# Two output projections of a fused eight-block transformer stack: five outputs over seven feature blocks beside the last mixer, their eighth block inside the sixth output

## The chip, the cores and the metric
The kernel runs on one core of a Trainium2 chip. The core has a matrix engine (TensorE, PE in the profile; its weight loads are PEld), a vector engine (VectorE, DVE), a scalar engine (ScalarE, ACT) and GpSimd (POOL); SyncE (SP) issues the DMAs. Engines run their own instruction streams in order and wait for one another by semaphores. The metric is the device time of one execution in microseconds; lower is better.

## What is computed
Two models of two layers follow one another on 512 latent tokens of width 1024. All data are kept with features on the 128 partitions, in KC = 8 feature blocks of 128, and tokens along the free axis. The part around the change is the first model:

```
layer 0:  x_lat += g1 * (attention(h_lat, h_ctx) @ na_w_o)      # 512 latent and 256 context tokens
          x_ctx += cg1 * (attention_ctx(h_ctx) @ na_w_o)
          x_lat += g2 * swiglu(norm(x_lat)), x_ctx likewise
layer 1:  x_lat += g1 * (readout(gated scans of h) @ hg_w_o)    # latent only from here
          x_lat += g2 * swiglu(norm(x_lat))
```

The attention has 16 heads, taken in eight pairs; a pair yields one feature block of 128 of the attention's output (o_lat, o_ctx). The second mixer has 8 heads of 128, and each yields one feature block of y_lat. So the input blocks of each output projection become ready one after the other, and the last one only when the last mixer is done.

## The kernel before
A weight matrix is taken in pieces. A piece is one block of 128 output features over kn feature blocks of the input (kn = 8 in most); its weights are one DMA of 512 KB into a ring of three w_raw buffers. Each product is computed with a high and a low part of both operands: ACT casts w_raw to w_high (event `w`, L1185), DVE subtracts to get w_low (L1514), and per feature block PE makes three products with 512 latent columns (L914 to L916) and, where there is context, three with 256 (L919 to L921). w_high and w_low are rings of two, by the piece's number: ACT's cast for piece n waits until piece n-2 and all before are done (`s_mm`).

The order of the work is written out by a planner, the class `Schedule`, as one list of events; every engine walks the same list and does its share of each event. `piece` first lays down the preload of its own weights, then the products of the piece before it (which were staged), and stages its own. The epilogue of a piece (event `epi`) comes behind the second block of the next piece's products, followed by an adaptive-modulation row (`ada`, two DVE products of 128x1024 with the weights of another DMA, L1526), one per piece in layer 0. `preload(2)` converts the first two pieces of the next stage in advance. `flush` lays down what is staged, with its epilogue.

Mixers are generators. `start_background(mixer, slots)` lets a mixer with a given number of steps be spread evenly over so many slots; each feature block but the first of a piece is a slot (`tick`), and a step is put behind its products. `end_background` lays down all steps that are left, one after the other. The attention mixer of a pair has 32 steps (transposes of v, the norms of q and k, nine empty ones, then five rounds of scores, transposes of the probabilities and value products), the second mixer 34 (gates, logarithms, scans, then seven levels of a decomposition of the scores: differences on POOL, exponentials on ACT, products on DVE, score products on PE three levels later; then the output and its norm).

In both mixer stages the mixer of head i lies beside the pieces of head i+1: 21 slots for the 32 attention steps, 35 for the 34 of the second. The last attention mixer starts when nothing is left beside it, so that all its steps are laid down by `end_background`. The last one of the second stage starts behind its second forget-gate piece with a rate of 34 steps in 28 slots; 14 slots are there (pieces v and g), the other half of the steps comes behind.

Then come `preload(2)`, eight events `to_h` (ACT casts block k of o_lat and o_ctx, or of y_lat, into h_high, L1224, L1225, L1228; DVE subtracts to h_low, L1573, L1575, L1578) and the eight output pieces. Their epilogue adds gate times product to x_lat and x_ctx on DVE (L1588, L1590), and `feed` adds ACT's squares (`sq`) and POOL's running sum of them (L1951) for the next norm. `flush`, `preload(2)` and `norm` follow: `ssum` (PE, L944 for the running sum and L947 for the last square), `rstd` (ACT), and per block the modulation and the split into h_high and h_low (L1560, L1166, L1566), which the first FFN products wait for.

Of the kernel before, what the change touches and what calls it, by code (L numbers as in the profile page):

```python
# [59 lines left out]

TABLES = {ACT.Exp: "natural_log_exp_and_others", ACT.Ln: "natural_log_exp_and_others", ACT.Silu: "silu_and_others",
# [3 lines left out]
class Piece:  # L65


    def __init__(self, src, kn, rhs, epi, gate):
        self.src, self.kn, self.rhs, self.epi, self.gate = src, kn, rhs, epi, gate
        self.ctx = rhs in ("hc", "uc")  # L70


class Schedule:
# [81 lines left out]
    def piece(self, src, kn, rhs, epi, gate=None, first=False, then=None):  # L155
        n = len(self.pieces)
        self.pieces.append(Piece(src, kn, rhs, epi, gate))
        if n >= self.loaded:
            self.preload()

        def products():
            if first:
                self.run_epilogues()
            for k in range(kn):
                self.ev("mm", n, k)
                if k == 1:
                    self.run_epilogues()
                    self.flush_late()
                    self.fill_ada(self.ada_rate)
                if k >= 1:  # L170
                    self.tick()
            self.pending.append(finish)
# [213 lines left out]
    def main(self):  # L386
# [8 lines left out]
        self.interleave([self.na_pieces(i) for i in range(KC)], [(self.na_mixer(i), 32) for i in range(KC)], 3 * (KC - 1))  # L395
        self.preload(2)
        for k in range(KC):
            self.ev("to_h", 0, k)
        for m in range(KC):
            self.piece(io["na_o"][m], KC, "hc", ("res", m, 0, 2, 1), gate=("to_h", 0) if m == 0 else None)  # L400
        self.flush()
        self.preload(2)
# [7 lines left out]
                        tail_chunks=4 * (KC - 1), after=2)  # L410
        self.preload(2)
        for k in range(KC):
            self.ev("to_h", 1, k)
        for m in range(KC):
            self.piece(io["hg_o"][m], KC, "h", ("res", m, 1, 2, 3), gate=("to_h", 1) if m == 0 else None)
        self.flush()
        self.preload(2)
# [37 lines left out]
def build(nc, io):  # L455
    ctx = ExitStack()
    with ctx:
# [128 lines left out]
        s_th, s_tl = sem("s_o_high"), sem("s_o_low")  # L586
        s_uh, s_ul = sem("s_u_high"), sem("s_u_low")
# [29 lines left out]
        by_epi = {p.epi: n for n, p in enumerate(pieces)}  # L617

# [41 lines left out]


# [32 lines left out]
        def mix_uses(ev):  # L694
            kind = ev[0]
            v = nth[ev]
            if kind == "shm":
                return []
            if kind == "shift":
# [100 lines left out]
        def _(e):  # L800
# [19 lines left out]
            for ev in plan:  # L820
                kind = ev[0]
                if kind == "w":
# [3 lines left out]
                    e.dma_start(raw[slot][:, 0:p.kn * P], p.src).then_inc(s_raw[slot], 16)  # L826
# [48 lines left out]
        def _(e):  # L875
# [6 lines left out]
            for ev in plan:  # L882
# [41 lines left out]

                elif kind == "shift":
# [231 lines left out]
        def _(e):  # L1157
# [10 lines left out]
            for ev in plan:  # L1168
# [17 lines left out]
                elif kind == "sq":  # L1186
# [4 lines left out]
                    else:  # L1191
                        n = by_epi[("res", k, *RES_OF[s], s)]
                        e.wait_ge(*(ctx_free if HAS_CTX[s] else lat_free)[n])
# [26 lines left out]
                elif kind == "to_h":  # L1220
                    _, which, k = ev
                    if which == 0:
# [278 lines left out]
        def _(e):  # L1501
# [5 lines left out]
            for ev in plan:  # L1507
# [71 lines left out]

                elif kind == "epi":  # L1580
# [541 lines left out]
```

## Time and profile before

| | us |
|---|---|
| median of 3 runs | 3602.36 (3601.1 to 3602.77) |
| the profiled execution | 3599.17 |
| its span | 3597.4 |
| PE busy in it | 3328.5 |
| DVE busy | 1747.3 |
| ACT busy | 1273.6 |
| POOL busy | 399.4 |
| weight products over h (L914 alone, 2752 of them) | 1136.0 |

The chain that ended last is PE for 80% of the span, DVE for 7%, ACT for 5%, POOL for 4%. The mean granted clock of PE is 0.974 of full speed. A matmul's duration in the rows contains its latency; back to back, its successor starts earlier than it ends. A row of the timeline gives the start, the duration, the engine, the line, output and inputs, and in brackets how long the engine was idle before it and what ended that.

### The profile page before, as it was taken

The page shows a single profiled execution, that of the slowest core. Times are in us where ns is not written, and L with a number is a line of the kernel's source. Part 1 is how long each engine was busy: PE and PEld are TensorE (multiplying, and loading weights), DVE is VectorE, ACT ScalarE, POOL GpSimd, SP SyncE. Part 2 cuts the span into 40 slices and gives each one's busy share as a digit, 9 for nine tenths or more (in the row PEclk, how much of TensorE's full clock was granted, in tenths as well). Part 3 has the DMA queues.
Part 4 walks back from the last instruction along what each step waited for, and adds up shares of the span by engine and source line. Part 5 has one row for each costly group of instructions (what it writes and reads, how often), then busy time and mean ns, then how long its engine had stood idle before and what let it go on. Part 6 is the DMA issues. An engine that isn't in the chain of part 4 may idle for free.

```text
span 3597.4 us, 42857 instructions
## 1 busy us (share of the span) xinstructions
PE 3328.5 (93%) x17064; PEld 2756.1 (77%) x17064; DVE 1747.3 (49%) x2602; ACT 1273.6 (35%) x1965; POOL 399.4 (11%) x400
## 2 busy tenths in 40 slices
PE   3888878999999999997999999999989999999898
PEld 3777757888887778776788878887768788877686
DVE  3666667755533676765533334343333333433333
ACT  2444443212123465554322233333332333333322
POOL 1011001000001253533000000001100000011000
PEclk7999999999999999998999999999999999999999
DMA  5322213665621211111333322222223222222132
GB/s 175 86 68 64 68 47 112 193 195 191 194 91 47 64 48 48 48 42 43 101 94 95 93 96 70 76 74 79 69 67 100 91 81 72 69 83 76 53 97 85
DMA packets 107974, 318.75 MB, mean 89 GB/s; under 512 B 28160, under 2 KB 29568, under 8 KB 107264
## 3 DMA queue, kind: packets, MB, share of 16 engines
q1 hardware_dynamic: 107776, 316.00, 28.3%
q8 instruction: 137, 2.24, 0.3%
q14 instruction: 61, 0.50, 0.0%
HBM read 313.86 MB, written 2.10 MB: 88 GB/s over the span
## 4 chain that ended last, share of the span: by engine, by line
PE 80%; DVE 7%; ACT 5%; POOL 4%; issue 3%; DMA 1%; SPq 0%; DVEq 0%; ACTq 0%
PE bank L914 20%; PE bank L916 20%; PE bank L915 20%; PE bank L919 3%; PE bank L921 3%; PE bank L920 3%; PE bank L1108 1%; DVE tmp L1560 1%; PE bank L1127 1%; PE bank L1137 1%; POOL hg_d L1994 1%; ACT L1165 1%; PE bank L1009 1%; POOL hg_d L1995 1%; PE bank L982 1%
## 5 line engine op out<-in xcount | busy, mean ns | idle before, releaser
L914 PE MATMUL bank<-h_high_lat,w_high 128*128 128x512 f32 x2752 | 1136.0, 413 | 84.5 <-DVE h_low_ctx L1566 34.6
L1514 DVE TENSOR_TENSOR w_low<-w_raw,w_high 128x1024 fp32r<-128x1024 f32 (+2 forms) x440 | 537.3, 1222 | 1125.2 <-ACT w_high L1185 1123.8
L916 PE MATMUL bank<-h_high_lat,w_low 128*128 128x512 f32 x2752 | 1082.6, 393 | 0.0
L915 PE MATMUL bank<-h_low_lat,w_high 128*128 128x512 f32 x2752 | 1082.5, 393 | 0.0
L1185 ACT CAST w_high<-w_raw 128x1024 fp32r<-128x1024 f32 (+2 forms) x440 | 451.1, 1027 | 1335.0 <-PE bank L916 858.8
L914 PEld LDWEIGHTS bank<-h_high_lat,w_high 128*128 128x128 f32 x2752 | 523.0, 190 | 195.7 <-issue 63.6
L916 PEld LDWEIGHTS bank<-h_high_lat,w_low 128*128 128x128 f32 x2752 | 522.4, 190 | 113.1
L915 PEld LDWEIGHTS bank<-h_low_lat,w_high 128*128 128x128 f32 x2752 | 524.6, 191 | 79.3 <-issue 8.2
L1526 DVE SCALAR_TENSOR_TENSOR ada_product<-w_raw,c_rows 128x1024 f32<-128x1024 f32 x192 | 246.0, 1281 | 65.5 <-DMA w_raw<-in_ada_w_dram 53.8
L1951 POOL TENSOR_TENSOR rstd<-rstd,square 128x512 f32<-128x512 f32 (+1 forms) x42 | 64.8, 1544 | 1496.9 <-ACT square L1166 1496.6
L919 PE MATMUL bank<-h_high_ctx,w_high 128*128 128x256 f32 x800 | 225.6, 282 | 0.0
L920 PE MATMUL bank<-h_low_ctx,w_high 128*128 128x256 f32 x800 | 225.5, 282 | 0.0
L921 PE MATMUL bank<-h_high_ctx,w_low 128*128 128x256 f32 x800 | 225.3, 282 | 0.0
L919 PEld LDWEIGHTS bank<-h_high_ctx,w_high 128*128 128x128 f32 x800 | 151.2, 189 | 33.1
L920 PEld LDWEIGHTS bank<-h_low_ctx,w_high 128*128 128x128 f32 x800 | 151.2, 189 | 32.9
L921 PEld LDWEIGHTS bank<-h_high_ctx,w_low 128*128 128x128 f32 x800 | 153.8, 192 | 0.0
L916 PE MATMUL bank<-u_high_lat,w_low 128*128 128x512 f32 x352 | 139.0, 395 | 0.0
L915 PE MATMUL bank<-u_low_lat,w_high 128*128 128x512 f32 x352 | 138.9, 395 | 0.0
L914 PE MATMUL bank<-u_high_lat,w_high 128*128 128x512 f32 x352 | 138.3, 393 | 0.4 <-DVE u_low_lat L1610 0.4
L2006 POOL TENSOR_TENSOR ret_rot<-head_in,cos 128x512 f32<-128x512 f32 x16 | 23.4, 1461 | 974.7 <-DVE ya_low L1886 689.1
L1166 ACT ACTIVATE na_p<-bank,na_stat 128x512 f32<-128x512 f32 (+1 forms) x96 | 58.9, 616 | 150.0 <-DVE na_stat L1678 131.1
L1165 ACT ACT_TABLE_LOAD x64 | 82.1, 1283 | 71.1 <-DVE att_stat L1864 48.8
(244 smaller groups left out, 4285.4 us busy)
## 6 DMA issues: line engine op xcount, KB each, us to landing
w_raw<-in_w_in_dram SPq DMA_DIRECT2D x176, 512.0 KB, 3.5
w_raw<-in_ada_w_dram SPq DMA_DIRECT2D x88, 512.0 KB, 3.9
w_raw<-in_ffn_in_dram SPq DMA_DIRECT2D x88, 512.0 KB, 3.6
w_raw<-in_w_ada_dram SPq DMA_DIRECT2D x48, 512.0 KB, 4.5
w_raw<-in_hg_in_dram SPq DMA_DIRECT2D x40, 512.0 KB, 3.5
w_raw<-in_ffn_out_dram SPq DMA_DIRECT2D x32, 512.0 KB, 3.6
w_raw<-in_qkv_dram SPq DMA_DIRECT2D x24, 512.0 KB, 3.6
w_raw<-in_proj_ret_dram SPq DMA_DIRECT2D x16, 512.0 KB, 3.5
```

The source lines that it names most:

```text
L914: e.matmul(lat_b, a, h[:, k, :], start=start, stop=False)
L915: e.matmul(lat_b, a, l[:, k, :], start=False, stop=False)
L916: done = e.matmul(lat_b, b, h[:, k, :], start=False, stop=stop)
L919: e.matmul(ctx_b, a, h[:, k, :], start=start, stop=False)
L920: e.matmul(ctx_b, a, l[:, k, :], start=False, stop=False)
L921: done = e.matmul(ctx_b, b, h[:, k, :], start=False, stop=stop)
L1165: e.preload_act_table_set(name)
L1166: return e.activation(out, in_, func, **kw)
L1185: e.copy(w_hi[n % 2][:, 0:p.kn * P], raw[slot][:, 0:p.kn * P]).then_inc(s_hi, 1)
L1514: e.tensor_tensor(w_lo[n % 2][:, 0:w], raw[slot][:, 0:w], w_hi[n % 2][:, 0:w].bitcast(F32), ALU.subtract).then_inc(s_lo, 1)
L1526: e.scalar_tensor_tensor(ada_x[:, :], raw[slot][:, :], 1.0, cb[:, c, :], ALU.mult, ALU.mult, accum_out=mod[layer][:, idx, k, c:c + 1]).the ...
L1951: e.tensor_tensor(RS[:, 0:w], RS[:, 0:w], sqr[(k - 1) % 2][:, 0:w], ALU.add).then_inc(s_gadd, 1)
```

## The change
Both projections now have three parts. `project` lays down the first five outputs (EARLY = 5) as pieces over the first seven feature blocks; they are the tail of the mixer stage, and the last mixer is spread over their slots (30 in the first projection; 44 in the second, which are the 14 of before and 30). Their `to_h` events for blocks 0 to 6 stand ahead of them, behind the last piece of the mixer stage, and ACT waits before the first until that piece is done, since h_high is its input. The epilogues add the seven-block sums to x as usual, but feed no squares.

`project_last` then ends the mixer, lays down `to_h` for block 7 and computes the sixth output over all eight blocks. The eighth weight blocks of outputs 0 to 4 are one piece of their own, loaded by one DMA of runs of 128 numbers. Behind blocks 2 to 6 of the sixth output stands one event `last` each: the three (in the first projection six) products of block 7 for one of the five outputs, into a mixer bank, and DVE's add of the result to x_lat (and x_ctx), followed by the squares of that output. Behind the fifth, the weights of the seventh output are preloaded. Outputs 7 and 8 follow, with `preload(2)` ahead of the last output's products instead of behind them.

```diff
+EARLY = 5
@@ interleave
-    def interleave(self, producers, mixers, chunks, tail=(), tail_chunks=0, after=-1):
+    def interleave(self, producers, mixers, chunks, tail=(), tail_chunks=0, after=-1, keep=False):
...
             for p in tail:
                 p()
-            self.end_background()
+            if not keep:
+                self.end_background()
             return
...
+    def project(self, which):
+        W, layer = (self.io["na_o"], 0) if which == 0 else (self.io["hg_o"], 1)
+
+        def early(m):
+            if m == 0:
+                self.preload()
+                self.flush()
+                for k in range(KC - 1):
+                    self.ev("to_h", which, k)
+            self.piece(W[m, :, 0:(KC - 1) * P], KC - 1, "hc" if which == 0 else "h", ("res", m, layer, 2, None),
+                       gate=("to_h", which) if m == 0 else None)
+
+        return [lambda m=m: early(m) for m in range(EARLY)]
+
+    def project_last(self, which, s):
+        W, layer = (self.io["na_o"], 0) if which == 0 else (self.io["hg_o"], 1)
+        rhs = "hc" if which == 0 else "h"
+        n = len(self.pieces)
+        self.pieces.append(Piece(W[0:EARLY, :, (KC - 1) * P:KC * P].rearrange("m p c -> p m c"), EARLY, rhs, ("last", which), None))
+        self.preload()
+        self.flush()
+        self.preload()
+        self.end_background()
+        self.ev("to_h", which, KC - 1)
+
+        def between(k):
+            m = k - 2
+            if 0 <= m < EARLY:
+                self.ev("last", which, m, n)
+                self.feed(s, m)
+            if m == EARLY - 1:
+                self.preload()
+
+        self.piece(W[EARLY], KC, rhs, ("res", EARLY, layer, 2, s), between=between)
+        self.staged.pop(0)()
+        for m in range(EARLY + 1, KC):
+            self.piece(W[m], KC, rhs, ("res", m, layer, 2, s))
+        self.preload(2)
+        self.flush()
@@ main, first projection
-        self.interleave([self.na_pieces(i) for i in range(KC)], [(self.na_mixer(i), 32) for i in range(KC)], 3 * (KC - 1))
-        self.preload(2)
-        for k in range(KC):
-            self.ev("to_h", 0, k)
-        for m in range(KC):
-            self.piece(io["na_o"][m], KC, "hc", ("res", m, 0, 2, 1), gate=("to_h", 0) if m == 0 else None)
-        self.flush()
-        self.preload(2)
+        self.interleave([self.na_pieces(i) for i in range(KC)], [(self.na_mixer(i), 32) for i in range(KC)], 3 * (KC - 1),
+                        tail=self.project(0), tail_chunks=5 * (KC - 2), keep=True)
+        self.project_last(0, 1)
@@ main, second projection
-                        tail_chunks=4 * (KC - 1), after=2)
...
+                        tail=self.project(1), tail_chunks=2 * (KC - 1) + 5 * (KC - 2), after=2, keep=True)
+        self.project_last(1, 3)
@@ PE
+                elif kind == "last":
+                    _, which, m, n = ev
+                    a, b = w_hi[n % 2][:, m * P:(m + 1) * P], w_lo[n % 2][:, m * P:(m + 1) * P]
+                    if m == 0:
+                        e.wait_ge(s_lo, n + 1)
+                        e.wait_ge(s_tl, 2 * KC if which == 0 else 3 * KC)
...
+                    done.then_inc(s_last if m < EARLY - 1 else s_mm, 1)
@@ ACT, to_h
+                    if k == 0:
+                        e.wait_ge(s_mm, to_h_from[which])
@@ DVE
+                elif kind == "last":
+                    _, which, m, n = ev
+                    layer = which
+                    e.wait_ge(s_mod, mod_nth[(layer, 2)])
+                    e.wait_ge(*((s_last, (EARLY - 1) * which + m + 1) if m < EARLY - 1 else (s_mm, n + 1)))
+                    e.wait_ge(*lat_free[by_epi[("res", m, layer, 2, None)]])
+                    e.scalar_tensor_tensor(XL[:, m, :], mix_bank[(ev, 0)][:, :], mod[layer][:, 2, m, 0:1], XL[:, m, :],
+                                           ALU.mult, ALU.add).then_inc(s_ll, 1)
...
```

## Rows read from the trace of the kernel before

**Rows 1.** The page: busy time, share of the span, instructions.
```profile
PE 3328.5 (93%) x17064; PEld 2756.1 (77%) x17064; DVE 1747.3 (49%) x2602; ACT 1273.6 (35%) x1965; POOL 399.4 (11%) x400
```

**Rows 2.** Copies that close a head: all by line, and one in the timeline.
```profile
L1697 DVE COPY o_ctx<-bank x8: 424/425/425, 169.2 to 518.6; 128x256 f32<-128x256 f32 x8
...
477.85 0.42 DVE L1697 COPY o_ctx<-bank 128x256 f32<-128x256 f32 x1 [2.73 <-PE bank L1009]
...
L1809 DVE SCALAR_TENSOR_TENSOR y_lat<-tmp,vectors,rstd x8: 751/752/754, 1254.8 to 1653.6; 128x512 f32<-128x512 f32 x8
```

**Rows 3.** Windows: length, busy PE, PEld, DVE, ACT, POOL, PE's clock, DMA.
```profile
428.70:469.90 41.20, 36.55 (x250) 29.76 (x249) 28.24 (x59) 17.31 (x37) 5.14 (x7) 1.00 0.16 38
477.70:522.40 44.70, 25.09 (x180) 17.93 (x179) 25.61 (x57) 24.12 (x56) 4.35 (x6) 0.84 0.03 6
522.40:590.00 67.60, 67.60 (x385) 59.82 (x386) 50.19 (x67) 16.34 (x29) 11.06 (x6) 0.98 0.38 121
...
1209.00:1611.70 402.70, 370.37 (x2246) 322.34 (x2245) 282.48 (x400) 229.00 (x358) 190.38 (x210) 0.98 0.15 47
...
1658.60:1704.00 45.40, 45.31 (x193) 37.41 (x194) 16.24 (x20) 11.79 (x15) 7.72 (x6) 0.96 0.25 79
```

**Rows 4.** Timeline of PE, the first projection's first product.
```profile
522.40 0.77 PE L914 MATMUL bank<-h_high_lat,w_high 128*128 128x512 f32 x1 [3.81 <-DVE h_low_ctx L1575]
```

**Rows 5.** Timeline of PE, last head of the second mixer.
```profile
1619.80 1.51 PE L1020 MATMUL bank<-matrices,hg_v 128*128 128x128 f32 x6 [4.48 <-issue]
...
1658.69 0.77 PE L914 MATMUL bank<-h_high_lat,w_high 128*128 128x512 f32 x1 [7.82 <-DVE h_low_lat L1578]
```

**Rows 6.** Timeline of ACT and DVE, what precedes the first conversions.
```profile
476.81 1.20 ACT L1251 COPY na_v<-bank 128x256 f32<-128x256 f32 x4 [0.36 <-PE bank L921]
...
521.24 0.69 DVE L1573 TENSOR_TENSOR h_low_lat<-o_lat,h_high_lat 128x512 fp32r<-128x512 f32 x1
```

**Rows 7.** The page, costliest groups: the two halves of a weight conversion.
```profile
L1514 DVE TENSOR_TENSOR w_low<-w_raw,w_high 128x1024 fp32r<-128x1024 f32 (+2 forms) x440 | 537.3, 1222 | 1125.2 <-ACT w_high L1185 1123.8
...
L1185 ACT CAST w_high<-w_raw 128x1024 fp32r<-128x1024 f32 (+2 forms) x440 | 451.1, 1027 | 1335.0 <-PE bank L916 858.8
```

**Rows 8.** Timeline, all engines, end of the first projection.
```profile
583.05 1.22 DVE L1526 SCALAR_TENSOR_TENSOR ada_product<-w_raw,c_rows 128x1024 f32<-128x1024 f32 x1
...
584.25 1.83 POOL L1951 TENSOR_TENSOR rstd<-rstd,square 128x768 f32<-128x768 f32 x1 [4.28 <-ACT square L1166]
584.32 2.86 DVE L1526 SCALAR_TENSOR_TENSOR ada_product<-w_raw,c_rows 128x1024 f32<-128x1024 f32 x1
...
590.26 0.75 DVE L1588 SCALAR_TENSOR_TENSOR x_lat<-bank,mod,x_lat 128x512 f32<-128x512 f32 x1 [2.87 <-PE bank L921]
...
591.44 0.63 ACT L1166 ACTIVATE square<-x_lat 128x512 f32<-128x512 f32 x1 [7.33 <-DVE x_ctx L1590]
...
599.62 0.77 PE L914 MATMUL bank<-h_high_lat,w_high 128*128 128x512 f32 x1 [5.63 <-DVE h_low_ctx L1566]
```

**Rows 9.** Timeline of PE: the first work after two idle stretches.
```profile
1561.19 0.51 PE L914 MATMUL bank<-h_high_lat,w_high 128*128 128x512 f32 x1 [2.65 <-DVE w_low L1514]
...
2610.37 3.29 PE L1127 MATMUL bank<-ret_rot 128*128 128x512 f32 x4 [3.37 <-issue]
```

**Rows 10.** Timeline of DVE and ACT, last head of the second mixer.
```profile
1618.26 1.10 DVE L1760 TENSOR_TENSOR hg_qb<-hg_qb,hg_q 128x512 f32<-128x512 f32 x1
...
1626.51 1.72 DVE L1788 SCALAR_TENSOR_TENSOR hg_x<-hg_d,lower_bound,hg_k 128x256 f32<-128x256 f32 x2
...
1629.92 1.78 DVE L1788 SCALAR_TENSOR_TENSOR hg_x<-hg_d,lower_bound,hg_k 128x256 f32<-128x256 f32 x2
...
1650.95 1.28 ACT L1165 ACT_TABLE_LOAD   x1 [1.32 <-PE bank L1072]
...
1654.56 3.38 DVE L1514 TENSOR_TENSOR w_low<-w_raw,w_high 128x1024 fp32r<-128x1024 f32 x2 [0.18 <-ACT w_high L1185]
```

**Rows 11.** Timeline of PE, first FFN product of layer 1.
```profile
1711.31 0.77 PE L914 MATMUL bank<-h_high_lat,w_high 128*128 128x512 f32 x1 [4.58 <-DVE h_low_lat L1566]
```

More of the change, by code:

```diff
@@ L69, in __init__ @@
         self.src, self.kn, self.rhs, self.epi, self.gate = src, kn, rhs, epi, gate
-        self.ctx = rhs in ("hc", "uc")
+        self.ctx = rhs in ("hc", "uc") and epi[0] != "last"
 class Schedule:
@@ L153, in preload, with piece @@
             self.loaded += 1
-    def piece(self, src, kn, rhs, epi, gate=None, first=False, then=None):
+    def piece(self, src, kn, rhs, epi, gate=None, first=False, then=None, between=None):
         n = len(self.pieces)
@@ L171, in products @@
                     self.tick()
+                if between is not None:
+                    between(k)
             self.pending.append(finish)
@@ L586, in build @@
         s_th, s_tl = sem("s_o_high"), sem("s_o_low")
+        s_last, s_ll, s_lc = sem("s_last_bank"), sem("s_last_lat"), sem("s_last_ctx")
         s_uh, s_ul = sem("s_u_high"), sem("s_u_low")
@@ L617, in build @@
         by_epi = {p.epi: n for n, p in enumerate(pieces)}
+        for n, p in enumerate(pieces):
+            if p.epi[0] == "last":
+                lat_free[n] = lat_free[n - 2]
+        to_h_from = {p.gate[1]: n for n, p in enumerate(pieces) if p.gate is not None and p.gate[0] == "to_h"}
         raw_use, raw_before, lines = {}, {}, []
@@ L659, in build, with res_done @@
         RES_OF = {1: (0, 2), 2: (0, 5), 3: (1, 2), 4: (1, 5), 5: (2, 2), 6: (3, 2)}
+        def res_done(s, k):
+            if s == 1 and k < EARLY:
+                return s_lc, k + 1
+            if s == 3 and k < EARLY:
+                return s_ll, EARLY + k + 1
+            return (ctx_free if HAS_CTX[s] else lat_free)[by_epi[("res", k, *RES_OF[s], s)]]
         s_nmask, s_panel = sem("s_na_mask"), [sem("s_panel0"), sem("s_panel1")]
@@ L698, in mix_uses @@
                 return []
+            if kind == "last":
+                return [(s_ll, v), (s_lc, v)] if ev[1] == 0 else [(s_ll, v)]
             if kind == "shift":
@@ L825, in _ @@
                     free_raw(ev)
-                    e.dma_start(raw[slot][:, 0:p.kn * P], p.src).then_inc(s_raw[slot], 16)
+                    dst = raw[slot][:, 0:p.kn * P]
+                    if p.epi[0] == "last":
+                        dst = dst.rearrange("p (m c) -> p m c", c=P)
+                    e.dma_start(dst, p.src).then_inc(s_raw[slot], 16)
                 elif kind == "ada":
@@ L923, in _ @@
                         done.then_inc(s_mm, 1)
+                elif kind == "last":
[4 more added lines that the diff above has]
+                        e.wait_ge(s_tl, 2 * KC if which == 0 else 3 * KC)
+                    h, l = HhL[:, KC - 1, :], HlL[:, KC - 1, :]
+                    out = bank(ev, 0)[:, :]
+                    e.matmul(out, a, h, start=True, stop=False)
+                    e.matmul(out, a, l, start=False, stop=False)
+                    done = e.matmul(out, b, h, start=False, stop=True)
+                    if which == 0:
+                        h, l = HhC[:, KC - 1, :], HlC[:, KC - 1, :]
+                        out = bank(ev, 1)[:, 0:CTX]
+                        e.matmul(out, a, h, start=True, stop=False)
+                        e.matmul(out, a, l, start=False, stop=False)
+                        done = e.matmul(out, b, h, start=False, stop=True)
+                    done.then_inc(s_last if m < EARLY - 1 else s_mm, 1)
                 elif kind == "shift":
```

14 lines of the change are left out of this document (5 added, 9 removed).

## Prediction
> **What bounds the kernel now.** I read the page first: TensorE (PE) is busy for 93% of the span [rows 1], so time is lost only where PE stands still or runs at its lower clock. Then the copies that close a head, the busy time by windows, and PE's timeline around the two output projections; behind each idle stretch, the lines of ScalarE (ACT), VectorE (DVE) and GpSimd (POOL) that end it.
>
> In the neighbourhood attention a head pair takes 51.4 us: its o_ctx copy comes at 169.2 first and at 477.85 six heads later [rows 2]. Its three pieces are dense work: the eight output pieces of the same shape take 67.6 us [rows 3], whose start runs at 1.2 GHz (0.77 us for the first product, [rows 4]) and loses about 1.4 (an estimate: some 3 us at half speed); that leaves 66.2, so 8.28 per piece and 1.035 per feature block. The mixer beside them adds 51.4 - 24.8 = 26.6 us. PE is idle for 11% of the window in a steady head [rows 3]; I take 6 to 7 us of the 51.4, so 19.3 to 20 us is PE's mixer work. The last mixer has nothing beside it: between 477.7 and 522.4 (44.7 us) PE shows 25.1 us busy, at a granted clock of 0.84 [rows 3]. That is what the change can fill.
>
> In the second mixer a head takes 57.0 us (the y_lat writes, 1254.8 to 1653.6 in seven intervals, [rows 2]). Its pieces are two lat-only ones and three with context: eight lat-only pieces take 45.4 us [rows 3], less 1.9 of slow start 5.44 each, so 2 x 5.44 + 3 x 8.28 = 35.7. The mixer adds 21.3; PE is idle for 8% (370.4 busy of 402.7, [rows 3]), 4.6 us, so 16.7 us of PE work. Its last head is half covered: from the end of the last g product (1615.3, which is 1619.80 less 4.48) to the projection's first (1658.69) PE waits for a chain over POOL, ACT and DVE [rows 5].
>
> **First projection, part by part.** Gone: the 44.7 us and the slow start, 1.4: 46.1. What comes back:
> - The seven early conversions need the last v product to be finished. ACT copies na_v first (1.20 us from 476.81), then converts; DVE subtracts (0.69 lat, 0.4 context) [rows 6]. First product at about 479.8: 2.1 us of idle PE. Later blocks come at DVE's pitch of about 0.95, under PE's 1.035. Bounds 1.5 and 3.8, the latter being today's wait at 522.40 [rows 4].
> - The mixer's PE work: 19.3 us, beside 35 blocks. 32 steps lie in 30 slots instead of 21, so that each score has more time before its transpose. Idle inside: at most today's 7, at least about 1. DVE has per piece one w_low (1.22, [rows 7]), two ada products (2.4) and now the two residuals (1.2, [rows 8]); I take 4.5, nearer to today's row.
> - Wait before the sixth output. Its weights may be converted only when the fifth early piece has left their half of the w ring, and then PE has nothing but the mixer's last value product (about 1.1). ACT 1.03 and DVE 1.22 [rows 7], with the o_ctx copy (0.42, [rows 2]) and the residuals (1.2) ahead of w_low on DVE: about 3.9, less the value product: 2.8. Least 1.2 (cast and w_low alone), most 5.
> - The spread products: five blocks move, none is added. Their ten DVE adds, the squares and POOL's add (1.83, [rows 8]) lie beside 2.07 us of PE per step; the conversion of block 7 lies beside the sixth output's first three blocks. All 0. The load of the eighth blocks, in runs of 512 bytes, is issued a whole piece ahead; no row has such a load, and 7 us for it would still be hidden.
> - Wait before the seventh output: its weights take the ring slot of the spread piece, which ends one block (1.04) before the sixth output's end. Then 1.2 on DVE, the squares 1.0 on ACT, 1.03 and 1.22: 4.6 with hand-overs, less 1.04: 3.6. Bounds 1.3 (if the cast came straight behind) and 5.
> - The end. Two preloads now stand ahead of the last output's products. For the second, ACT waits until the last product is done, and behind its w_low DVE has the residuals of the seventh output, an ada pair and the residuals of the eighth. Today the last square starts 1.4 us after the last product (591.44, [rows 8]). Then: cast and w_low to +2.3, residuals to +3.4, first ada +4.6, second ada beside POOL's add (2.86 at 584.32, [rows 8]) +7.4, residuals +8.6. The norm, and the first FFN product (599.62 today), come 7.2 us later. Least 2.3 (w_low alone), most 9.
>
> The Trainium skill, SBUF — State Buffer, section "Who interferes with whom", says that a DVE instruction with two SBUF inputs and a GpSimd instruction that reads SBUF exclude one another. This trace agrees: 1.22 us for the ada product alone at 583.05, 2.86 beside the POOL add [rows 8]. Without such a lock that end would cost 5.6; the sum goes by the row.
>
> A stall of over 3 us also costs clock: after 2.65 us of idle PE in dense work the next product took 0.51, at full clock; after 3.37 us four products of 128x512 took 3.29, at the lower level [rows 9]. So 1.4 more for the stall of 3.6, nothing for 2.1 and 2.8.
> Back: 2.1 + 19.3 + 4.5 + 2.8 + 3.6 + 1.4 + 7.2 = 40.9. Gain: 46.1 - 40.9 = **5.2 us**.
>
> **Second projection.** Gone: 43.4 us (1615.3 to 1658.7), 1.9 of slow start, and 0.9 for a group of score products that lies beside the g piece today and moves behind it (34 steps in 44 slots, no longer in 28): 46.2. Back:
> - The conversions stand on DVE behind the gate and scan steps (which end at 1619.3 today, [rows 10]), on ACT behind the same exponentials, and one w_low more lies before them. First product at about 1622.3, 8 us behind the last g product; today PE waits 4.5 there [rows 5]. 8.0, and 1.8 for the clock. Bounds 4.5 and 10.
> - The mixer: 16.7. Idle inside: DVE's levels take 3.4 us today (1626.51 to 1629.92, [rows 10]); PE would ask for one every 2.8, but a level is prepared three ahead of its use. 4.0; bounds 0 and 12.
> - Wait before the sixth output: the last statistics product stands two slots before the end; then ACT's table load 1.28 [rows 10], logarithm and exponential 1.2, cast 1.03, w_low 1.22, less 1.4 of products: 3.4, and 1.7 for the clock. Bounds 1.2 and 5.
> - Before the seventh: 0.75 + 0.63 + 1.03 + 1.22 and 0.3 of hand-overs, less 0.68: 3.2, between the two gaps of [rows 9]: half a slow start, 0.9.
> - The end: cast and w_low to +2.3, residual and square of the seventh output, POOL's add 1.3, then both statistics products, where only the second is left today: 4.3 later than now (first FFN product 1711.31, [rows 11]). No ada here. Bounds 2.3 and 5.
>
> 8.0 + 1.8 + 16.7 + 4.0 + 3.4 + 1.7 + 3.2 + 0.9 + 4.3 = 44.0. Gain **2.2 us**. The same rule of the skill (same page, same section) speaks against the change here: the subtractions have two SBUF inputs and now fall beside POOL's differences. The trace shows it: two w_low beside POOL took 3.38, not twice 1.22 [rows 7, 10]. For the first conversion and the w_low ahead it is in the 8.0, some 1.5 us; without it the wait would be 6.5.
>
> Sum: 5.2 + 2.2 = 7.4 us. The profiled execution took 3599.17 with a span of 3597.4; the median of the runs shown is 3602.36, 3.2 above. 3599.2 - 7.4 + 3.2 = 3595.0.
>
> **Rivals.**
> 1. The mixers hide as a whole: idle inside falls to 1 and 0 us instead of 4.5 and 4.0: 7.5 less, 3587.5. For it: fewer steps per slot than in any head now. Against: DVE has more beside them.
> 2. DVE becomes the bound, and the time is longer than before: 3606. Place: the levels of the second mixer's last head. Every early piece puts w_low (1.22, 1.7 beside POOL) and a residual (0.75) into the chain that fills DVE already, and seven subtractions (7 us beside POOL) stand ahead of it. 7 levels x 3.5 + 7 + 12.5 for the pieces + 8 for the output = 52 from 1622.3, against 1622.3 + 1.8 + 23.8 + 16.7 + 4.0, that is 46.3: +5.7, and the two slots and the wait behind it +2.7; and in the first mixer today's 7 us of idle stay (+2.6). It decides once a level with its share of a piece's work (3.4 + 1.8 each 1.7 levels) outlasts the lead of three levels, some 8 us. Against: DVE has gaps outside the levels.
> 3. What is filled is given back by the waits at the joints: the ends cost 9 and 5, the waits for w_low 5 each, the clock falls at each: 6.5 more, 3601.5. For it: these waits are certain in kind and only their sizes open. Against: each is made of durations of rows.
>
> **Chances.** Forecast 0.42, rival 1 0.23, rival 2 0.17, rival 3 0.18. The forecast's own range is 3590 to 3600. Runs of this kernel can't tell less than 0.2% (7.2 us) from no change, and the forecast lies at that edge: some 0.24 of its share counts as faster, rival 1 with all of its: 0.47. Slower by over 0.2% needs rival 2 with more than its price, 0.10; within, 0.43. Range 3584 to 3607: from rival 1 with shorter waits to rival 2.
>
> **What would show it.** Right: the two long stretches of sparse PE work are gone; in their place stand four waits for w_low (2.8, 3.6, 3.4, 3.2 us), one of 8 us behind the last g product, and 17 and 12 us from the last product to the FFN (9.6 and 7.4 today). Wrong: if the early pieces hold over 10 us of idle in either mixer, if the seventh output has no wait, or if at the end DVE's residual of the seventh output doesn't lie behind a w_low. The forecast fails as a whole if these stretches together are off by more than 7 us.

## The result and the profile after

The changed kernel takes 3609.28 us (median of 12 executions, 3603.88 to 3612.34); the kernel before, on the same chip, 3602.05 (12, 3598.63 to 3604.77). The ratio is 1.0021, 95% interval 1.0013 to 1.0028: about 7 us slower, where 7.4 us faster was forecast. The profiled execution has a span of 3605.4 us against 3597.4. Of all executions reported below one, of e5, took 3861.26 us at a granted clock of 0.837; its ratio leaves it out.

The page's line of busy times:
```profile
PE 3335.9 (93%) x17064; PEld 2758.1 (76%) x17064; DVE 1750.9 (49%) x2619; ACT 1272.9 (35%) x1967; POOL 401.5 (11%) x400
```
PE executes as many instructions as before and is 7.4 us longer busy with them than in [rows 1]; the mean granted clock is 0.973 against 0.974. A share of 93% on both sides doesn't tell where the time went; the windows do.

**Four stretches.** Four PE products divide the span: the first behind norm 0, the first FFN product of layer 0 ("FFN 0"), the first product behind norm 2, and the first FFN product of layer 1 ("FFN 1"). Microseconds, from the timelines; A holds the first projection, C the second, B and D are the same work in all kernels:
```
                 start    A: to FFN 0  B: to norm 2  C: to FFN 1  D: rest    span
before           84.51    515.11       566.45        545.24       1886.1    3597.4
after            82.86    520.63       567.55        545.61       1888.7    3605.4
```
The first projection is 5.5 us longer (5.2 shorter was forecast), the second 0.4 longer (2.2 shorter forecast). The other 2.1 us lie where the code is the same; the runs below show that stretches of unchanged code differ by 2 to 6 us from one execution to another.

**First projection.** Timeline of PE after: first early product, the two longest waits between the early products, sixth output, seventh output, last product, norm, FFN 0 (the brackets hold the idle time before the instruction and what ended it):
```profile
479.08 0.47 PE L970 MATMUL bank<-h_high_lat,w_high 128*128 128x512 f32 x1 [1.93 <-DVE h_low_ctx L1650]
...
488.68 1.10 PE L1038 MATMUL bank<-square,matrices 128*128 128x512 f32 x2 [1.46 <-issue]
...
522.39 1.12 PE L1066 MATMUL bank<-matrices,na_p 128*128 128x128 f32 x4 [3.15 <-ACT na_p L1240]
...
550.25 0.50 PE L970 MATMUL bank<-h_high_lat,w_high 128*128 128x512 f32 x1 [2.71 <-DVE w_low L1589]
...
568.26 0.50 PE L970 MATMUL bank<-h_high_lat,w_high 128*128 128x512 f32 x1 [4.25 <-DVE w_low L1589]
...
586.39 0.28 PE L977 MATMUL bank<-h_high_ctx,w_low 128*128 128x256 f32 x1
593.12 2.90 PE L1018 MATMUL bank<-rstd,matrices 128*128 128x512 f32 x4 [6.45 <-POOL rstd L2038]
...
603.49 0.76 PE L970 MATMUL bank<-h_high_lat,w_high 128*128 128x512 f32 x1 [5.51 <-DVE h_low_ctx L1641]
```
The waits before the sixth and the seventh output are there, both ended by w_low (2.8 and 3.6 us forecast), and 1.93 before the first early product (2.1 forecast). The early products themselves last from 479.1 to 547.5. Windows after: the whole early stretch, its start and its middle, and the last two pieces (columns as in [rows 3]):
```profile
479.10:547.50 68.40, 62.24 (x388) 50.76 (x388) 47.35 (x94) 27.81 (x60) 4.38 (x6) 0.93 0.24 73
...
479.10:484.10 5.00, 5.00 (x21) 4.40 (x22) 5.00 (x11) 5.00 (x12) 0.00 (x0) 0.66 0.01 3
...
522.30:530.00 7.70, 7.61 (x40) 5.82 (x40) 4.09 (x12) 2.56 (x7) 0.31 (x1) 0.61 0.14 55
...
568.30:586.60 18.30, 18.30 (x96) 15.98 (x96) 7.32 (x8) 1.99 (x3) 1.83 (x1) 0.91 0.36 116
```
68.4 us, where the forecast had 60.0 (36.2 + 19.3 + 4.5). 6.2 of them are idle PE. And the clock, for which the forecast had charged nothing here, is at 0.66 in the first 5 us and at 0.61 behind the wait of 3.15.

What VectorE does ahead of that wait, timeline of DVE after:
```profile
515.84 1.09 DVE L1589 TENSOR_TENSOR w_low<-w_raw,w_high 128x896 fp32r<-128x896 f32 x1 [1.12 <-ACT w_high L1259]
516.85 0.74 DVE L1675 SCALAR_TENSOR_TENSOR x_lat<-bank,mod,x_lat 128x512 f32<-128x512 f32 x1
517.51 0.47 DVE L1677 SCALAR_TENSOR_TENSOR x_ctx<-bank,mod,x_ctx 128x256 f32<-128x256 f32 x1
517.90 1.22 DVE L1601 SCALAR_TENSOR_TENSOR ada_product<-w_raw,c_rows 128x1024 f32<-128x1024 f32 x1
...
519.16 1.23 DVE L1601 SCALAR_TENSOR_TENSOR ada_product<-w_raw,c_rows 128x1024 f32<-128x1024 f32 x1
...
520.31 0.43 DVE L1760 TENSOR_TENSOR bank<-bank,na_bias 128x256 f32<-128x256 f32 x1
```
A whole piece's work (w_low, two residuals, two ada products: 4.5 us) runs without a gap, and the mixer's score add, for whose softmax the transposes on PE wait, comes only behind it.

Ahead of the projection one more term shows. Copies of o_ctx that close the last two heads with pieces beside them: the first one before (its successor is in [rows 2]), then both after, with the conversion that lies between them only in the changed kernel, timeline of DVE:
```profile
427.12 0.42 DVE L1697 COPY o_ctx<-bank 128x256 f32<-128x256 f32 x1 [2.72 <-PE bank L1009]
```
```profile
425.45 0.42 DVE L1784 COPY o_ctx<-bank 128x256 f32<-128x256 f32 x1 [2.73 <-PE bank L1083]
...
458.55 1.09 DVE L1589 TENSOR_TENSOR w_low<-w_raw,w_high 128x896 fp32r<-128x896 f32 x1
...
477.20 0.42 DVE L1784 COPY o_ctx<-bank 128x256 f32<-128x256 f32 x1 [2.73 <-PE bank L1083]
```
51.75 us, against 50.73 before. The first early piece has its weights converted beside the last v piece, where there was no conversion before: 1.0 us. All earlier heads take 51.6 us in every trace. This last one takes 50.7 in before, e2 and e8, which lack the conversion, 51.8 in after, e3, e5, e6, e9 and e10, and 52.8 in e1, e4 and e7, whose clock between 467 and 477 is 0.83, where after has 1.00.

The end, timeline of DVE after:
```profile
587.79 1.23 DVE L1589 TENSOR_TENSOR w_low<-w_raw,w_high 128x1024 fp32r<-128x1024 f32 x1 [7.03 <-ACT w_high L1259]
588.93 0.75 DVE L1675 SCALAR_TENSOR_TENSOR x_lat<-bank,mod,x_lat 128x512 f32<-128x512 f32 x1
...
589.98 1.22 DVE L1601 SCALAR_TENSOR_TENSOR ada_product<-w_raw,c_rows 128x1024 f32<-128x1024 f32 x1
...
591.25 2.82 DVE L1601 SCALAR_TENSOR_TENSOR ada_product<-w_raw,c_rows 128x1024 f32<-128x1024 f32 x1
...
594.20 0.75 DVE L1675 SCALAR_TENSOR_TENSOR x_lat<-bank,mod,x_lat 128x512 f32<-128x512 f32 x1
```
The last residual comes 7.5 us behind the last product, in the order that was forecast: w_low, the seventh output's residual, ada, ada beside POOL's add, the eighth's. From the end of the last product (586.67) to FFN 0 it is 16.8 us, against 9.6.

**Second projection.** Timeline of PE after: end of the last g product, first early product, sixth and seventh output, last product, FFN 1; and the windows of the early stretch and of the last two pieces:
```profile
1620.38 0.39 PE L972 MATMUL bank<-h_high_lat,w_low 128*128 128x512 f32 x1
1626.97 0.77 PE L970 MATMUL bank<-h_high_lat,w_high 128*128 128x512 f32 x1 [6.20 <-DVE h_low_lat L1653]
...
1675.62 0.80 PE L970 MATMUL bank<-h_high_lat,w_high 128*128 128x512 f32 x1 [3.91 <-DVE w_low L1589]
...
1689.79 0.80 PE L970 MATMUL bank<-h_high_lat,w_high 128*128 128x512 f32 x1 [3.68 <-DVE w_low L1589]
...
1703.28 0.39 PE L972 MATMUL bank<-h_high_lat,w_low 128*128 128x512 f32 x1
...
1716.65 0.76 PE L970 MATMUL bank<-h_high_lat,w_high 128*128 128x512 f32 x1 [4.02 <-DVE h_low_lat L1641]
```
```profile
1627.00:1671.60 44.60, 41.75 (x233) 34.86 (x233) 33.67 (x52) 18.79 (x25) 18.12 (x24) 0.96 0.17 52
...
1689.80:1703.70 13.90, 13.87 (x48) 10.89 (x48) 2.96 (x3) 1.68 (x2) 1.28 (x1) 0.79 0.12 38
```
From the last g product to FFN 1 it is 95.9 us; before it was 96.0 (1615.3 to 1711.31). The head is filled as meant, and the four waits (6.2 at the start, 3.9, 3.7, and 5.6 more at the end) take it back together with the clock behind them.

### The profile page after: what moved, and what is told of

It reads as the page before. It is cut to its first block, busy times and chain, and to the rows that moved or that the text cites. A ratio compares the mean times of both kernels' runs of the same rounds, so it can differ in the third digit from the quotient of the medians.

```text
span 3605.4 us, 42894 instructions
## 1 busy us (share of the span) xinstructions
PE 3335.9 (93%) x17064; PEld 2758.1 (76%) x17064; DVE 1750.9 (49%) x2619; ACT 1272.9 (35%) x1967; POOL 401.5 (11%) x400
## 4 chain that ended last, share of the span: by engine, by line
PE 79%; DVE 8%; ACT 5%; POOL 4%; issue 3%; DMA 1%; SPq 0%; DVEq 0%; ACTq 0%; POOLq 0%
PE bank L970 20%; PE bank L972 20%; PE bank L971 20%; PE bank L975 3%; PE bank L977 3%; PE bank L976 3%; PE bank L1182 1%; DVE tmp L1635 1%; PE bank L1201 1%; PE bank L1211 1%; POOL hg_d L2082 1%; POOL hg_d L2081 1%; PE bank L1083 1%; ACT L1239 1%; PE bank L1164 1%
## 5 line engine op out<-in xcount | busy, mean ns | idle before, releaser
L1589 DVE TENSOR_TENSOR w_low<-w_raw,w_high 128x1024 fp32r<-128x1024 f32 (+3 forms) x442 | 539.6, 1222 | 1129.2 <-ACT w_high L1259 1127.9
L1259 ACT CAST w_high<-w_raw 128x1024 fp32r<-128x1024 f32 (+3 forms) x442 | 451.5, 1023 | 1326.5 <-PE bank L972 856.5
L970 PEld LDWEIGHTS bank<-h_high_lat,w_high 128*128 128x128 f32 x2742 | 522.3, 190 | 211.1 <-issue 71.5
```

Source lines behind the costliest of these rows:

```text
L970: e.matmul(lat_b, a, h[:, k, :], start=start, stop=False)
L1259: e.copy(w_hi[n % 2][:, 0:p.kn * P], raw[slot][:, 0:p.kn * P]).then_inc(s_hi, 1)
L1589: e.tensor_tensor(w_lo[n % 2][:, 0:w], raw[slot][:, 0:w], w_hi[n % 2][:, 0:w].bitcast(F32), ALU.subtract).then_inc(s_lo, 1)
```

## The experiments

After the result two theories stood against each other. The first: the loss is in the first projection, inside the early stretch, because VectorE's queue there holds a piece's work and two ada products ahead of the mixer's steps. The rivals: it lies in the second projection's last head (VectorE as the bound, the forecast's second rival), or at the joints, above all at the ends, where two weight conversions stand ahead of the last residuals. Each edit below is one to the changed kernel where nothing else is said. "Before" in each is the kernel before, timed on the same chip together with it.

**One projection at a time.** e1 keeps the old second projection, e2 the old first.
```
e1:  interleave(na ..., tail=project(0), keep=True); project_last(0, 1)      # changed
     interleave(hg ..., tail_chunks=4 * (KC - 1)); preload(2); eight pieces   # as before
e2:  the other way round
```


> Only the first projection is changed, the second is as before. By the profiles the first stretch (last v product to first FFN product) takes 127.4 us after against 122.9 before, the second 96.0 against 96.0. Theory P (the profile's places are the whole): 4 to 5 us slower than before, nearly all that the change costs. Rival Q (the cost lies evenly, or outside both stretches, as a drift of 3 to 4 us that the profile shows behind them): 2 to 4 slower here and as much with the second alone.

> Only the second projection is changed. Theory P: no difference from before (within 2 us), its stretch stays at 96 us. Rival Q: 3 to 4 us slower. The forecast had 2 us faster.

Measured: e1 3610.47 (9 executions), ratio 1.0027 [1.0017, 1.0037]; e2 3599.63 (11), ratio 0.9998 [0.9989, 1.0006]. Before: 3600.36. The loss is in the first projection, all of it; the second is worth nothing either way. The forecast's second rival falls: the second mixer doesn't become the bound. e2's heads close 50.72 us apart where the changed kernel has 51.75, which puts the extra conversion's 1.0 us on the first projection.

**The preloads behind the last epilogue.**
```
         for m in range(EARLY + 1, KC):
             self.piece(W[m], KC, rhs, ("res", m, layer, 2, s))
-        self.preload(2)
         self.flush()
+        self.preload(2)
```


> As after, but in both projections the two preloads stand behind the last output's products and epilogue, as before the change. Theory P: the ends cost 7.2 and 4 us, so from last product to FFN 17.0 falls to 9.7 and 13.0 to 9; in all 10 to 11.5 us less than after, that is 3 to 4 faster than before. Rival: DVE and ACT then have the conversions behind the last square and the norm waits for them, so that only 4 to 6 are won and it ends even with before.

Measured: 3591.85 (9), ratio to before 0.9976 [0.9966, 0.9986]. Timeline of e3, seventh output's first product and FFN 0 on PE, and DVE between them:
```profile
571.25 0.50 PE L970 MATMUL bank<-h_high_lat,w_high 128*128 128x512 f32 x1 [4.25 <-DVE w_low L1589]
...
589.79 0.75 DVE L1675 SCALAR_TENSOR_TENSOR x_lat<-bank,mod,x_lat 128x512 f32<-128x512 f32 x1 [2.87 <-PE bank L977]
...
592.87 2.36 DVE L1589 TENSOR_TENSOR w_low<-w_raw,w_high 128x1024 fp32r<-128x1024 f32 x2 [1.94 <-ACT w_high L1259]
...
599.14 0.77 PE L970 MATMUL bank<-h_high_lat,w_high 128*128 128x512 f32 x1 [5.63 <-DVE h_low_ctx L1641]
```
The residual now comes as soon as the product ends, and both w_low fit into the norm's own wait. From the seventh output to FFN 0 it takes 27.9 us instead of 35.2; from the seventh output of the second projection to FFN 1, 20.1 instead of 26.9. That is 7.3 + 6.8 = 14.1, of 17.4 us between the medians, 16.2 by the two ratios, and 15.7 between the two profiles; the rest lies in other parts, where executions of the same code differ too. The order of two lines decides the sign of the whole change.

**No ada products beside the early pieces of the first projection.** The rows left out are made in the first feed-forward.
```
             if m == 0:
                 self.preload()
                 self.flush()
+                self.ada_rate = 0
 ...                                    # project_last, before end_background()
+        self.ada_rate = 1
```


> As after, but the five adaptive-modulation rows that lie beside the five early pieces of the first projection are left to the FFN behind it (all rows are still computed). Theory D (DVE's queue: w_low, residuals and two ada products in a row, 4.5 us, stand ahead of the scores and hold the mixer): the early stretch of 68.4 us falls by 5 to 8, the 3.15 us wait for na_p goes and the clock stays up; the FFN pays nothing or up to 2. Rival C (the stretch is PE's own work plus the hand-overs inside the mixer): it falls by less than 2.

Measured: 3602.10 (11), ratio 1.0002 [0.9993, 1.001], 7.2 under the changed kernel, 6.8 by the two ratios. Windows of e4: the whole early stretch and its first 5 us; and the score add on DVE behind the same w_low (1.09 at 515.98) and residuals as above:
```profile
481.70:542.30 60.60, 57.82 (x388) 47.55 (x388) 35.49 (x74) 27.85 (x60) 4.39 (x6) 1.00 0.13 40
...
481.70:486.70 5.00, 5.00 (x32) 4.47 (x32) 5.00 (x11) 5.00 (x12) 0.00 (x0) 1.00 0.01 3
```
```profile
517.66 0.47 DVE L1679 SCALAR_TENSOR_TENSOR x_ctx<-bank,mod,x_ctx 128x256 f32<-128x256 f32 x1
518.05 0.42 DVE L1762 TENSOR_TENSOR bank<-bank,na_bias 128x256 f32<-128x256 f32 x1
```
60.6 us for the same 388 instructions that took 68.4. Of the 7.8, 3.4 are idle PE (6.16 against 2.78) and 4.4 are busy PE (62.24 against 57.82), at a clock of 0.93 against 1.00. No wait on PE in this stretch is over 1 us. But how a stretch with ada products divides into waits and lower clock differs between executions, and its length hardly does. e3 has the same early stretch as the changed kernel, with 1.00 in its first 5 us and behind its wait of 3.15. Window of that stretch in e3 and its first long wait on PE; then the window in e9 (below), which has no ada products and starts at 0.66:
```profile
481.20:549.00 67.80, 59.58 (x388) 48.38 (x388) 47.35 (x94) 27.97 (x60) 4.38 (x6) 0.97 0.24 74
```
```profile
490.83 2.05 PE L1038 MATMUL bank<-square,matrices 128*128 128x512 f32 x2 [3.03 <-issue]
```
```profile
482.00:543.50 61.50, 59.27 (x388) 48.86 (x388) 35.56 (x74) 27.99 (x60) 4.40 (x6) 0.97 0.12 40
```
67.8 us at nearly full clock, of which 8.2 are idle: the faster start only makes the first wait 3.03 instead of 1.46. So the lower clock is not what made the stretch long. Traces with like starts give the price of the ada products: starting at 0.66, 68.4 (after) against 61.5 (e9, e10); starting at 1.00, 67.8 and 67.9 (e3, e1) against 60.6 and 60.7 (e4, e6); 6.9 to 7.3 us. The edit takes out the products' weight loads too (DMA share 0.24 against 0.13), which no run does apart; w_low takes 1.09 with and without them, and the score add comes 2.4 us earlier, the length of two products, so that these 2.4 us are VectorE's queue. A as a whole is only 4.2 under the changed kernel in this profile, because e4's has the last head at 52.8 us and 1.5 us more of lower clock in the sixth output.

**The sixth output's weights ahead of the spread piece's.** The waits before the sixth output come from the order in the ring of two weight slots; here the sixth's conversion lies beside the fifth early piece, the spread piece's behind it.
```
+        n = len(self.pieces) + 1
+        self.piece(W[EARLY], KC, rhs, ("res", EARLY, layer, 2, s), between=between)
+        self.run_epilogues()
         self.pieces.append(Piece(W[0:EARLY, ...], EARLY, rhs, ("last", which), None))
         self.preload()
-        self.flush()
-        self.preload()
         self.end_background()
 ...                 # `between` no longer preloads; the counts of s_mm and s_last change with the order
```


> One edit to the changed kernel, in both projections: the sixth output's weights are converted ahead of the spread piece's, beside the fifth early piece; the spread piece's weights follow when the fifth early piece has left their slot, and are needed only three blocks into the sixth output; the seventh output's weights now wait for the end of the sixth output as a whole. Theory A (the waits at the joints are made by the slot order alone): the waits before the sixth output (2.71 and 3.91 us in the changed kernel) go, and with the second one the lower clock behind it, some 1.5 us; the waits before the seventh stay between 3 and 5 us. In all 7 to 10 us under the changed kernel, 3600 us, and about level with the kernel before. Theory B (the wait only moves): the sixth output's conversion stands in the queues of ScalarE and VectorE beside the fifth early piece, so it pushes back the mixer's last steps, and the seventh's wait grows by what the sixth's loses: less than 3 us under the changed kernel, 3607 us or more.

Measured: 3609.2 (11), ratio 1.0014 [1.0005, 1.0023]: level with the changed kernel. PE of e5, the seventh output of the first projection; the sixth (its spread products, L986) and seventh of the second:
```profile
571.53 0.77 PE L967 MATMUL bank<-h_high_lat,w_high 128*128 128x512 f32 x1 [6.54 <-DVE x_ctx L1674]
...
1679.58 0.47 PE L986 MATMUL bank<-h_high_lat,w_high 128*128 128x512 f32 x1 [2.23 <-DVE w_low L1586]
...
1692.21 0.76 PE L967 MATMUL bank<-h_high_lat,w_high 128*128 128x512 f32 x1 [5.55 <-DVE x_lat L1672]
```
The wait only moved: 2.71 + 4.25 = 6.96 became 6.54, and 3.91 + 3.68 = 7.59 became 2.23 + 5.55 = 7.78. Theory A is wrong. Two conversions have to wait for the end of a piece with two slots, in whatever order.

**Both mended, and all three.** e6 and e9 are the same kernel (preloads behind, no ada beside the early pieces), e7 has the sixth output's order as well.

> Both earlier single edits at once on the changed kernel: the two preloads of weights behind the last output's epilogue, and no modulation products beside the five early pieces of the first projection (they are made in the first feed-forward instead). Theory A (the two costs are separate: one lies at the end, the other inside the last mixer): 3609.3 less 17.4 (preloads behind) less 7.2 (no modulation products), about 3585 us, ratio to the kernel before 0.995 to 0.996. Theory B (they share VectorE's queue as one cost, so the second edit finds little left): 3590 to 3592 us, as with the preloads behind alone.

> The changed kernel with all three edits: sixth output's weights ahead of the spread piece's, preloads behind the last epilogue, no modulation products beside the early pieces of the first projection. If the three costs are separate: the sum of the three single gains, 3609.3 - 17.4 - 7.2 - 8 = 3577 us, ratio 0.993. If the waits at the joints only move: 3585 us, as without the reordering. From the second projection: the sixth output starts without a wait of over 2 us in both projections if the separate costs are right.

> The changed kernel with the preloads behind and no modulation products beside the early pieces, timed again: its first runs gave 3584.0 once and 3591.4 to 3593.4 four times. If the costs add, the median is nearer 3585 than 3592; if VectorE's queue holds them as one, 3590 to 3593 again. If the two values come back with a gap of some 8 us, the profile shows in which stretch it lies.

Measured: e6 3592.79 (5), 0.9964 [0.9951, 0.9976]; e9 3585.85 (5), 0.9966 [0.9953, 0.9978]; e7 **3582.50** (5, 3581.32 to 3584.41), 0.9942 [0.9929, 0.9954]. Before: 3602.77, 3600.47 and 3602.77. All three are faster than both kernels. The costs add within the noise (by the ratios e3 and e4 bring 0.45% and 0.19%, e6 and e9 0.57% and 0.55%): the profiles of e6 and e9 have A = 507.1 and 507.8, 8.0 and 7.3 under before, and C = 539.1 and 538.7, 6.2 and 6.5 under it. The ten executions of this kernel form two groups, 3584.0 to 3587.7 and 3591.4 to 3594.0; both profiles fell in the lower one, so where the upper one's 8 us lie is open. e7's profile has the span of theirs (3582.6), so that the reordering shows no gain in the profiles; its five executions are all low, which five can't settle.

**The first projection alone, mended.**
```
 e1 with the edits of e3 and e4
```


> Only the first projection is changed, with the preloads behind and no modulation products beside its early pieces; the second projection is as in the kernel before. By the terms measured so far: the changed kernel's first projection lost 5.5 us against the kernel before, the preloads take 7.3 of it back and the modulation products 7.2, so 9 us under the kernel before, 3592 to 3594 us. The same, were the second projection worth nothing, as with both projections; if the mended second projection is worth its 6 us, this kernel is 6 us slower than the one with both.

Measured: 3594.37 (11), 0.9983 [0.9974, 0.9992], 6.1 under before (3600.47) and 8.5 above e9, which was timed with it, or 6.1 by the two ratios. The first projection mended is worth 6 us, the second another 6 to 8.5. In the changed kernel the second was worth nothing because its end gave back its gain.

**A control: no ada beside the first five output pieces of the kernel before.**
```
         for m in range(KC):
+            self.ada_rate = 0 if m < 5 else 1
             self.piece(io["na_o"][m], KC, "hc", ("res", m, 0, 2, 1), ...)
```


> A control on the kernel before: no modulation products beside the first five output pieces of the first projection; they are made in the first feed-forward instead. The dispute is whether the 7 us which that edit brought on the changed kernel belong to the change. Theory D (the products cost only where the mixer's chain needs VectorE at the same time): in the kernel before those pieces have no mixer beside them, so nothing is gained, within 2 us of the kernel before. Rival (moving the products into the feed-forward is a gain by itself): 5 to 7 us faster, 3596 us.

Measured: 3600.64 (11), ratio 1.0003 [0.9994, 1.0012], A = 515.8 against 515.1. Eight ada products fewer stand beside the output pieces, and nothing is gained where no mixer runs beside. The 7 us belong to the change.

**All profiles by stretch**, as above:
```
                 start    A         B         C         D         span
before           84.51    515.11    566.45    545.24    1886.1    3597.4
after            82.86    520.63    567.55    545.61    1888.7    3605.4
e1 first only    83.93    523.66    567.48    548.57    1885.6    3609.2
e2 second only   83.95    515.35    566.45    544.59    1886.5    3596.8
e3 preloads      85.00    514.14    565.99    539.51    1885.1    3589.7
e4 no ada        83.85    516.44    567.88    545.69    1886.4    3600.3
e5 sixth first   84.14    524.14    566.66    542.74    1890.5    3608.2
e6 both          84.60    507.13    566.80    539.05    1884.6    3582.2
e9 both          84.35    507.77    567.13    538.73    1884.6    3582.6
e7 all three     84.72    506.77    566.25    538.86    1886.0    3582.6
e10 first, both  82.67    506.32    566.42    547.03    1888.9    3591.3
e8 control       84.00    515.82    566.69    545.49    1886.1    3598.1
```
Read down a column of unchanged code for the noise of one profile: D is 1884.6 to 1890.5, C of the old second projection 545.2 to 548.6. A of one and the same first projection is 520.6 (after) and 523.7 (e1).

## Why the prediction was wrong

By the profiles the miss is 15.4 us: 3590.0 forecast for the span, 3605.4 measured. 10.7 of it are in A, 2.6 in C, 2.1 outside both.

1. **Idle inside the first mixer: the step that failed.** "I take 4.5, nearer to today's row", beside 19.3 of mixer work and 36.2 of products: 60.0 in all; measured 68.4. The forecast had listed what DVE has per piece (w_low, two ada products, two residuals) and then taken the idle time from a steady head without asking how these stand in the queue. The pieces of a steady head carry no residuals, and PE's clock beside them is 1.00 [rows 3]. With residuals in front and two ada products behind, 4.5 us of piece work precede a mixer step. Taking out the ada products alone (e4) brings the stretch to 60.6; the control (e8) shows that they cost nothing beside pieces without a mixer. Whether the 7 us appear as waits (8.2 us idle in e3) or in part as lower clock (6.2 idle at 0.93 in the changed kernel) differs between executions. The mixer's own work was taken too low as well: 11% of 51.4 is 5.8 us of idle time, not "6 to 7", which leaves 20.8 of PE work, and even 7 would leave 19.6, not 19.3. At full clock e4 has 57.82 us of busy PE, 21.6 beside the 36.2 (part of it can be the latency that the rows contain), so 2.3 more than the sum had. The 8.4 us of the miss are then 2.3 of this, 1.7 of idle time and 4.4 of clock in the changed kernel, and by the same reckoning 2.3, 3.7 and 1.8 of 7.8 in e3. The forecast's own sign of failure, over 10 us of idle time in a mixer, didn't appear: it looked at idle time alone.
2. **A term that was missing: 1.0 us** for the conversion of the first early piece beside the last v piece. "What it moves" has to include the weights of what is moved: they are converted one piece earlier. At a lower clock the same head cost 2.1 (e1, e4, e7).
3. **Start 1.93 (2.1), before the sixth 2.71 (2.8), before the seventh 4.25 (3.6), clock behind it 18.30 - 16.56 = 1.7 (1.4), end 16.8 - 9.6 = 7.2 (7.2).** Each within 0.7 us, of the kind and with the releaser that was forecast. The 2.86 us of an ada product beside POOL's add [rows 8] returned as 2.82. e3 confirms the price of the end: 7.3 us come back there. With the other terms these leave 0.6 of the 10.7 us without a name. These two waits return within 0.01 us in every trace of the changed first projection that keeps the order of their weights; the clock doesn't, and A differs by 3.0 us between two executions of this code (after, e1), so that so small a remainder says little.
4. **Second projection: start 6.2 (8.0), early stretch 44.6 (46.3), before the sixth 3.91 (3.4), before the seventh 3.68 (3.2), end 13.0 - 7.4 = 5.6 (4.3).** Two terms beside these: the last two pieces took 13.9 us for 10.9 of dense work, so 3.0 of clock where 0.9 was forecast; and from norm 2 to the end of the last g product it is 449.7 us, 0.5 more than before, where 0.9 less was forecast. The signs nearly cancel (-1.8, -1.7, +0.5, +0.5, +1.3, +2.1, +1.4), which leaves 2.3 of the 2.6 us. The 8.0 was itself a slip: from 1615.3 to the 1622.3 that the forecast names it is 7.0, nearer to the 6.2 measured. e2, with a ratio of 0.9998, agrees that the second projection gains nothing.
5. **Rivals.** The third (given back at the joints, 3601.5) was nearest in kind: the four waits and two ends took 27.4 us back (2.71, 4.25, 3.91, 3.68, 7.2, 5.6), against 24.5 in the forecast (2.8, 3.6, 3.4, 3.2, 7.2, 4.3). These 2.9 us are a fifth of the miss. By its own terms (ends of 9 and 5, four waits of 5) that rival is 9.5 us over the forecast, 3604.5, not 6.5. The second was wrong in its place: it put the bound on VectorE into the second mixer, where DVE is free of ada products; it was the first mixer in which that happened, with 2.6 us as the price where the stretch ran 8.4 over the sum, 7 of them for the ada products.

The chance given to "slower by over 0.2%" (0.10) was too low for one more reason. The forecast was a difference of two sums of some 45 us each, with a dozen terms. The one that a single row of before couldn't size (a mixer beside pieces that carry residuals) had bounds of 1 and 7 us for the idle time, where 6.2 and 8.2 (e3) were measured, and no term for the clock inside the stretch.

## What to carry to other kernels

When work is pulled beside a chain that shares an in-order engine, count what stands in one run ahead of a step of the chain, not the engine's busy share (VectorE was at 69% here, 47.35 of 68.40), and move optional work out of that stretch first: 7 us here for work that was free elsewhere. Whatever prepares the next stage (weight conversions) goes behind the last epilogue that the stage's start depends on: 14 us here for the place of one line. The clock behind a wait has a price too, and it is a range: behind 3.68 us it cost 3.0 here, behind 3.15 us 3.0 (0.39 of 7.7) or nothing. Where a chain on another engine sets the pace it isn't added in full: with 0.66 at its start and 0.61 behind the 3.15 us (after) the early stretch was only 0.6 us longer than with 1.00 in both places (e3).

## What the runs showed of the hardware

The clock's answer to one and the same wait differs between executions. Windows of the first 5 us of early products, behind the same idle 1.93 us and the same products, in e9 and in e6:
```profile
482.00:487.00 5.00, 4.98 (x20) 4.33 (x21) 5.00 (x11) 5.00 (x12) 0.00 (x0) 0.66 0.01 3
```
```profile
480.85:485.85 5.00, 5.00 (x31) 4.48 (x32) 5.00 (x11) 5.00 (x12) 0.00 (x0) 1.00 0.02 3
```
20 instructions in one, 31 in the other: 1.2 GHz for part of the stretch, or 2.4 for all of it. After, e5, e9 and e10 show 0.66 there, e1, e3, e4, e6 and e7 1.00. The wait of 3.15 us (3.14 in e1) was followed over 7.7 us by 0.61 in the changed kernel (522.3) and 0.62 in e5, by 1.00 in e3 and e1. And behind the same wait of 2.71 us the sixth output with its spread products took, with the wait behind it, 18.0 us in the changed kernel, e9 and e10 (550.25 to 568.26), 19.5 in e1, e3, e4 and e6 (551.69 to 571.25 in e3). So one profile can mis-size a stall's price by 1.5 us, behind the 3.15 by 3.0, and a rule read from two stalls of one trace (2.65 us at full clock, 3.37 at the lower one, [rows 9]) is not a threshold. That such differences make the two groups of executions of e6 and e9 is possible and wasn't shown.
